# Two of four scalings of the delta-rule outputs: issued by POOL in place of VectorE

## What is computed

```python
def step(state, inp):                    # one chunk of the scan
    ...
    o = q_i * exp(dec_i) @ state + qk_i @ v_new
...
o = rms_norm(o, norm_g) * jax.nn.silu(z)  # per head, over its 128 columns
...
x = x + jnp.concatenate([y_a, y_b, y_c], axis=-1) @ w_out[l]
```

## Time and profile before

| | us |
|---|---|
| median of three runs | 1600.07 |
| the profiled execution | 1601.17 |
| its span in the trace | 1599.4 |
| PE busy | 1569.8 (98%) |
| DVE busy | 912.6 (57%) |
| ACT busy | 687.6 (43%) |
| POOL busy | 160.7 (10%) |
| share of the chain that ended last: PE | 94% |
| the same: DVE | 3% |

### The profile page before, as it was taken

How to read it: one execution, slowest core, us unless ns; L and a number is a source line. 1 busy time by engine, 2 the same in 40 slices (tenths; PEclk the granted TensorE clock), 3 DMA queues, 4 the chain that set the end, 5 groups by cost and what they waited for, 6 DMA issues and landing times.

```text
span 1599.4 us, 21522 instructions
## 1 busy us (share of the span) xinstructions
PE 1569.8 (98%) x7488; PEld 1303.5 (82%) x7488; DVE 912.6 (57%) x1318; ACT 687.6 (43%) x1001; POOL 160.7 (10%) x101
## 2 busy tenths in 40 slices
PE   6999999999999999999999999999999999999997
PEld 5888798888788888888788888888888888888886
DVE  5569887865754234443477666666456544444332
ACT  6735656554644223333255554444224434443221
POOL 3444585300000000000000000000000000000000
PEclk9999999999999999999999999999999999999998
DMA  7522100132132332322233333333232332232332
GB/s 271 187 80 67 54 1 28 40 106 79 45 114 92 105 99 85 103 98 88 82 96 95 96 97 98 99 99 106 93 104 79 106 103 93 92 105 78 101 97 79
DMA packets 45665, 149.50 MB, mean 93 GB/s; under 512 B 4784, under 2 KB 5936, under 8 KB 45616
## 3 DMA queue, kind: packets, MB, share of 16 engines
q1 hardware_dynamic: 42240, 139.90, 27.2%
q10 hardware_dynamic: 3376, 8.95, 1.6%
HBM read 146.47 MB, written 2.10 MB: 93 GB/s over the span
## 4 chain that ended last, share of the span: by engine, by line
PE 94%; DVE 3%; DMA 1%; ACT 1%; issue 0%; SPq 0%; DVEq 0%; ACTq 0%
PE acc L633 85%; DMA raw<-panels_a 1%; PE acc L878 1%; PE acc L918 1%; DVE c_acc L2127 1%; PE acc L890 1%; DVE w_lo L1995 1%; PE acc L1126 0%; PE acc L1147 0%; PE acc L807 0%; PE acc L949 0%; PE acc L708 0%; PE acc L974 0%; DVE x L2702 0%; DVE d_score_a L2219 0%
## 5 line engine op out<-in xcount | busy, mean ns | idle before, releaser
L633 PE MATMUL acc<-h_hi,w_hi 128*128 128x512 f32 x1248 | 491.3, 394 | 1.2 <-DVE w_lo L2003 0.7
L633 PE MATMUL acc<-h_hi,w_lo 128*128 128x512 f32 x1248 | 485.9, 389 | 0.0
L633 PE MATMUL acc<-h_lo,w_hi 128*128 128x512 f32 x1248 | 485.8, 389 | 0.0
L2003 DVE TENSOR_TENSOR w_lo<-raw,w_hi 128x1024 fp32r<-128x1024 f32 (+2 forms) x241 | 281.6, 1171 | 81.8 <-ACT w_hi L1397 57.7
L1397 ACT ACTIVATE w_hi<-raw 128x1024 fp32r<-128x1024 f32 (+2 forms) x241 | 242.0, 1008 | 177.2 <-PE acc L633 86.1
L633 PEld LDWEIGHTS acc<-h_hi,w_hi 128*128 128x128 f32 x1248 | 234.4, 188 | 51.6 <-issue 3.5
L633 PEld LDWEIGHTS acc<-h_hi,w_lo 128*128 128x128 f32 x1248 | 234.3, 188 | 49.1
L633 PEld LDWEIGHTS acc<-h_lo,w_hi 128*128 128x128 f32 x1248 | 234.5, 188 | 48.1 <-issue 1.0
L2405 DVE TENSOR_TENSOR x<-x,acc 128x512 f32 x32 | 22.0, 688 | 136.0 <-PE acc L633 135.5
L633 PE MATMUL acc<-u_hi,w_hi 128*128 128x512 f32 x256 | 99.6, 389 | 0.0
L633 PE MATMUL acc<-u_lo,w_hi 128*128 128x512 f32 x256 | 99.6, 389 | 0.0
(11 more groups left out here) (400 smaller groups left out, 2317.2 us busy)
## 6 DMA issues: line engine op xcount, KB each, us to landing
raw<-panels_a SPq DMA_DIRECT2D x112, 512.0 KB, 3.2
raw<-panels_b SPq DMA_DIRECT2D x68, 512.0 KB, 3.2
raw<-mix SPq DMA_DIRECT2D x48, 448.0 KB, 3.4
raw<-mix SPq DMA_DIRECT2D x16, 512.0 KB, 3.6
raw<-down SPq DMA_DIRECT2D x16, 384.0 KB, 3.1
raw<-down SPq DMA_DIRECT2D x16, 320.0 KB, 2.8
x<-xT ACTq DMA_DIRECT2D x4, 1024.0 KB, 9.5
x_rows<-xN ACTq DMA_DIRECT2D x2, 1024.0 KB, 9.3
```

What stands on the lines that cost most here:

```text
L633: mm = e.matmul(out, w[:, w_at:w_at + wn], a, start=first and n == 0, stop=last and n == 2)
L2003: TTn(lo, raw, k.w_hi[:, ahead.slot(w)].bitcast(F32), ALU.subtract).then_inc(k.s_split_done, 1)
```

## The change

The third and fourth scalings (chunks 2 and 3) are taken out of VectorE's turn 14 and put at the end of POOL's program, behind its last panel. POOL waits there for `go_inv` (L2363's reciprocal) and for each chunk's copy. The arithmetic, the operands and the semaphore that is counted up are the same; TensorE still waits for a count of 4.

```diff
@@ gpsimd_program
     for p in range(early, FRONT):
         split()
+    e.wait_ge(k.s_dve_once, DVE_ONCE["go_inv"])
+    for c in range(2, TT):
+        e.wait_ge(k.s_o_copied, c + 1)
+        r = k.tok[:, TOK_RG + c * HEADS:TOK_RG + (c + 1) * HEADS].unsqueeze(2).broadcast_to([P, HEADS, P])
+        g_o = til(k.g_o, c).rearrange("p (h t) -> p h t", h=HEADS)
+        TTn(g_o, g_o, r, ALU.mult).then_inc(k.s_go_scaled, 1)
@@ vector_program
             e.sem_inc(k.s_dve_once, 1)
             go_scaled(0)
             go_scaled(1)
-        if i == BEAT * TT + 2:
-            go_scaled(2)
-            go_scaled(3)
     go_norm(0)
```

## The result

| | before | changed |
|---|---|---|
| median of 17 runs, us | 1600.18 | 1603.42 |
| lowest to highest | 1599.14 to 1601.49 | 1601.61 to 1605.58 |
| the profiled execution | 1601.17 | 1604.40 |
| its span | 1599.4 | 1602.6 |

The ratio is 1.0020, with a 95% interval of 1.0012 to 1.0027: a small loss, but outside the noise and outside the forecast's range (1598.6 to 1602.2). All times compared here are of executions in the same, faster state; one later execution of before took 2667.71 us at a granted clock of 0.557 and is left out. One of the rivals took place, *POOL goes first*, and beside it something that no rival had priced.

The account below looks back on a forecast made before the run. PE was taken as the bound, busy 98% of the span. A VectorE delay of 1.05 us less a gain of 0.79 gave +0.26 us, moving the median from 1600.07 to 1600.3; the range was 1598.6 to 1602.2.

Parts of the forecast that it names:

- POOL goes first: Rival, chance 0.19: POOL gets in ahead of go_scaled(0), both VectorE scalings are pushed back, +1.4 us, 1601.4.
- What bounds the kernel, and the gain: PE bounds the kernel; removing two VectorE scalings ends PE's wait ahead of turn_outputs(2), worth 0.79 us.
- d: Delay of VectorE's work ahead of soften(14), carried one to one to turn(14); forecast 1.05 us, 0.72 to 1.5.
- POOL's duration: Each of POOL's two added 128x512 scalings was taken to last 1.28 us, bounds 0.95 to 1.74.
- POOL in time for `go_turn(0)`: POOL's second scaling ends near 310.4, before PE reaches go_turn(0) at 311.25 + d, so its duration costs nothing.
- The exclusion: At the scalings, a VectorE instruction with two SBUF tensors doesn't run beside a POOL one; go_scaled(1) pushed back 1.05 us.
- Who comes first: At 306.98, VectorE's go_scaled(0) was taken to go ahead of POOL's first scaling, which gets in at about 307.48.
- The rival's own sign: POOL gets in first if its record leads go_scaled(0) by clearly more than 0.02 us, say 0.05.
- The sum itself: Change of the span as delay ahead of soften(14) less gain: +0.26 us, from -0.07 to +0.7.
- d - 0.79: The span's change: VectorE's delay ahead of soften(14) less the 0.79 us gained at turn_outputs(2); +0.26 us.
- What a measurement can tell: For the whole kernel, a difference under 0.2% (3.2 us) can't be told from none; the forecast difference was 0.02%.
- The check given: Forecast wrong if PE waits ahead of go_turn(0), or the shift at the projection's first L633 isn't that at the end.

Follow-up runs that it names:

- again: The changed kernel run once more with no edit; 1603.60 us, ratio 1.0017 against before.
- PE filled: The changed kernel with 14 additional transposes on PE ahead of turn(14), their result unused; 1601.14 us, ratio 1.0003 against before.

## Why the prediction was wrong

- *What bounds the kernel, and the gain* (0.79): right. Measured -0.84 and -0.85 in place with d at 0, in three kernels.
- *POOL's duration* (1.28 taken, 0.95 to 1.74 as bounds): too high. It is 1.04, equal to L597's. POOL in time for `go_turn(0)`: right.
- *The exclusion*: right as a mechanism, read from two older collisions in the trace and now shown by the operand's place.
- *Who comes first*: wrong. The forecast took VectorE first at 0.50 against 0.19, from the earlier trace rows, where POOL's record led by 0.02 and VectorE still went ahead. There VectorE was at another such multiplication when POOL came, which the prediction didn't weigh:

```profile
168.80 0.69 DVE L2195 TENSOR_TENSOR g_xt<-const,g_xt 128x512 f32<-128x512 f32 x1
```

Here neither engine was at one, and POOL went first in all three traces of that order (changed, again, PE filled), each with a lead of 0.01. That this difference decides is argued and not tested. The rival's own sign, a lead of POOL's clearly above 0.02, was wrong as well. POOL first made d 1.73 and not 1.05; the rival's own d of 2.15 was too much, mostly because POOL's scalings are shorter than it took. This failure alone would have been small: +0.9, inside the range.
- *The sum itself*: "d - 0.79" is the step that failed, since it has no term for the clock. The prediction priced PE's wait at its length and took the work behind `turn(14)` as unchanged. The missing term measured 2.63 us in the first trace, 1.64 in the second, and 2.3 to 2.5 by the medians with and without PE filled. The rival *POOL goes first* was put at 1601.4 by the same sum and became 1603.4. The range ended at 1602.2 for want of this term.
- *What a measurement can tell*: the prediction took a difference under 0.2% for one that can't be told from none. With 17 executions of each the interval was 0.15% wide, and this 0.2% was told.
- *The check given* ("if the shift at the first L633 of the projection isn't that at the end"): the shift is 321.09 - 317.38 = 3.71 there and 3.2 at the end. The difference is the tail's 0.47, which differs between two traces of the changed kernel too. So this sign didn't point at the failed term.

A row of before could have warned. At its tail PE's gaps were only 0.71 and 0.74, with eight short products between them, and yet the four transposes behind them ran at half the clock, which the last line shows for their stretch:

```profile
1588.36 1.05 PE L1353 MATMUL acc<-const,sq 128*128 128x1 f32 x8 [0.71 <-ACT sq L1381]
1590.15 1.11 PE L1358 MATMUL acc<-const,tok 128*128 128x128 f32 x4 [0.74 <-DVE tok L1986]
...
1590.15:1591.20 1.05, 1.05 (x4) 0.71 (x4) 0.00 (x0) 0.00 (x0) 0.00 (x0) 0.50 0.00 0
```

## What to carry to other kernels

Work moved to POOL beside VectorE needs a start chosen against VectorE's instructions with two SBUF tensors; let it wait for their end, or give VectorE one operand from PSUM. Price a longer wait of TensorE twice: its length, and what runs behind it at half the clock. Before adding an instruction to an engine that TensorE waits for, add up the wait that results, and if it gets longer than those the trace shows at full clock, fill it or leave the change. One trace isn't enough to call a wait safe: look at the average clock of every execution too.

## What had not been expected of the hardware

A wait of TensorE far shorter than the work behind it changes that work's speed. PE's waits of 0.28 to 1.28 us here (behind an earlier one of 0.79) left the granted clock at 1.00 in the traces, and those of 1.80 to 2.48 came with 1.2 GHz for 3.4 to 5.5 us of the work behind them. The length of one wait alone doesn't settle it: the same wait of 1.8 us cost 2.63 us in one execution and 1.64 in another, at 0.95 and 1.28 three of eleven executions each had a lower average clock, and at the tail of before gaps of 0.71 and 0.74 were followed by a clock of 0.50. What exactly brings it down stays open.

And where VectorE and POOL come to SBUF within 0.01 us of each other, which of them goes first is worth far more than that: 0.14 us of POOL work ahead of its scalings turned the order round, and with it 2.5 to 2.7 us of the kernel.
